# The odd layer's scans and the way to their projection: tiles placed by lifetime, squares and roots moved into waits, heads released one by one

## The reference

```python
amat = eye(L) + dec_strict * (k @ k.T) * b            # unit lower triangular
u0 = solve(amat, v); w = solve(amat, exp(g) * k)
pmat = dec_incl * (q @ k.T) * b
u = u0 - w @ S                                        # S: the state carried into the chunk
o = exp(g) * (q @ S) + pmat @ u
S = exp(g_last) * S + (exp(g_last - g) * b * k).T @ u
```

## Time and profile before

| | us |
|---|---|
| median of 3 runs | 1511.68 |
| lowest and highest | 1505.21, 1513.31 |
| profiled execution | 1506.36 |
| its span in the trace | 1504.2 |
| TensorE, VectorE, ScalarE, GpSimd busy | 1316.4, 527.8, 339.2, 112.3 |

### The profile page before, as it was taken

The page is one execution under the profiler, slowest core; times in us unless marked ns, Lnnn a source line. Parts: engine busy times, 40 slices in busy tenths (PEclk is TensorE's granted clock), DMA queues, the critical chain, the costliest instruction groups (busy, mean ns, idle before and its releaser), DMA issues.

```text
span 1504.2 us, 17094 instructions
## 1 busy us (share of the span) xinstructions
PE 1316.4 (88%) x6506; PEld 815.0 (54%) x6506; DVE 527.8 (35%) x1090; ACT 339.2 (23%) x724; POOL 112.3 (7%) x136
## 2 busy tenths in 40 slices
PE   6999788999998997888999997978877989987883
PEld 3554675466884333333565557878776843333332
DVE  3010473332234111011557817677662341101014
ACT  2100314333231111111336213221223311111111
POOL 2400010000001111110000000000000011111100
PEclk9999897999999999999999999999797999999997
DMA  9951666166537999997342200100007379999971
GB/s 362 332 180 58 223 152 246 68 238 240 222 139 296 390 415 418 418 417 311 122 152 72 85 0 1 29 1 1 1 18 287 137 294 411 413 418 418 417 287 63
DMA packets 80726, 329.12 MB, mean 219 GB/s; under 512 B 18383, under 2 KB 19577, under 8 KB 55936
## 3 DMA queue, kind: packets, MB, share of 16 engines
q1 hardware_dynamic: 66224, 300.54, 51.3%
q0 software_dynamic: 14416, 27.41, 5.7%
HBM read 320.04 MB, written 29.53 MB: 232 GB/s over the span
## 4 chain that ended last, share of the span: by engine, by line
PE 63%; DMA 15%; DVE 13%; issue 6%; ACT 2%; SPq 0%; POOL 0%; DVEq 0%; ACTq 0%; POOLq 0%
PE psum L921 20%; PE psum L1266 12%; PE psum L1015 9%; DMA arena<-in_moe_w_up 6%; PE psum L1292 5%; PE psum L947 3%; DMA wide<-in_moe_w_up 3%; DMA ring<-in_moe_w_up 3%; PE psum L1010 2%; DMA ring<-in_ada_w 2%; DVE arena L2381 2%; DVE wide L2341 1%; PE psum L890 1%; DMA arena<-h_rows,slot_token 1%; PE psum L954 1%
## 5 line engine op out<-in xcount | busy, mean ns | idle before, releaser
L921 PE MATMUL psum<-wide,ring 128*128 128x384 f32 x704 | 240.6, 502 | 3.8 <-ACT wide L1580 1.9
L921 PEld LDWEIGHTS psum<-wide,ring 128*128 128x128 f32 x704 | 165.6, 239 | 70.9 <-issue 9.5
L1266 PE MATMUL psum<-arena 128*64 128x512 f32 x480 | 151.6, 624 | 19.0 <-DMA ring<-in_moe_w_up 11.7
L1266 PE MATMUL psum<-ring,arena 128*64 128x512 f32 x384 | 134.4, 624 | 8.9 <-DMA wide<-in_moe_w_up 4.7
L1015 PE MATMUL psum<-ring 128*128 128x128 f32 x872 | 114.6, 290 | 18.0 <-issue 8.7
L1015 PEld LDWEIGHTS psum<-ring 128*128 128x128 f32 x872 | 108.9, 203 | 23.2 <-issue 13.4
L921 PE MATMUL psum<-ring,wide 128*128 128x512 f32 (+2 forms) x336 | 116.1, 507 | 0.0
L2252 DVE TENSOR_TENSOR arena<-arena,psum 128x256 f32<-128x256 f32 x34 | 14.3, 421 | 286.7 <-ACT arena L1728 286.7
L1266 PEld LDWEIGHTS psum<-arena 128*64 128x64 f32 x480 | 47.0, 144 | 96.6 <-issue 96.4
L1266 PE MATMUL psum<-wide,arena 128*64 128x512 f32 x224 | 88.1, 610 | 7.5 <-DMA arena<-in_moe_w_up 7.5
L921 PEld LDWEIGHTS psum<-ring,wide 128*128 128x128 f32 x336 | 58.3, 190 | 57.2 <-issue 56.4
(11 more groups left out here) (505 smaller groups left out, 1717.5 us busy)
## 6 DMA issues: line engine op xcount, KB each, us to landing
ring<-in_ada_w SPq DMA_DIRECT2D x23, 2048.0 KB, 13.0
arena<-in_moe_w_gate SPq DMA_DIRECT2D x28, 1024.0 KB, 14.0
arena<-in_moe_w_up SPq DMA_DIRECT2D x28, 1024.0 KB, 20.4
arena<-in_moe_w_down SPq DMA_DIRECT2D x28, 1024.0 KB, 20.8
ring<-in_moe_w_gate SPq DMA_DIRECT2D x24, 1024.0 KB, 13.7
ring<-in_moe_w_up SPq DMA_DIRECT2D x24, 1024.0 KB, 18.8
ring<-in_moe_w_down SPq DMA_DIRECT2D x24, 1024.0 KB, 20.9
ring<-in_w_in_odd SPq DMA_DIRECT2D x7, 2048.0 KB, 8.5
```

The source lines that it names most:

```text
L921: ins = mm(out, lhs(k), rhs(k), start=(k == 0), stop=(k == n - 1))
L1266: ins = mm(psum[half, 2 + s, :].rearrange("p (w f) -> p w f", w=2), hg[s][:, k, half], buffers[UNITS[q][h] % BUFFERS][0][:, :, k, :], star ...
```

## The change

- The tiles are dealt anew. `passing` is ring slots 1 and 2, `lasting` the arena part and ring slot 0. G, E1, xdt, xw, EB and (all in slots 1 and 2) Uw and AT are passing; XT, X, LT, TT, Rg, U, y2 and PT are lasting. The first half of the output weights (slot 1) waits for both Y1 of the third pair to be read, the second (slot 2) for the 36th LT, the last.
- KS and O2 of the third pair move from step 6 to step 5; in both pairs the two KS come before the two O2. VectorE's part for O2 (`carried_out`) comes after the subtraction of step 6 in the second pair, and in step 6 ahead of it in the third.
- VectorE gates ysum ahead of O1's additions. ScalarE squares the first token tile's heads in step 3 of the third pair and takes their root in step 4; it squares ysum after the U copies, and the heads of tiles 2 and 1 each after its O1 addition.
- VectorE scales the first tile's heads before the second root; the other eight go head by head, and each head of both tiles releases one group of transposes.

```diff
@@ plan_jobs, the odd layer's pairs
-            elif n == 6 and c:
-                jobs += [(name, u) for u in two for name in ("KS", "O2")]
+            elif n == (6 if pair < 2 else 5) and c:
+                jobs += [(name, u) for name in ("KS", "O2") for u in two]
@@ build, tiles of the scans
-        parts = (carve(4096), ring[:, 0, :], ring[:, 1, :], ring[:, 2, :])
-        G = [parts[2 * w][:, 0:1024] for w in range(2)]
-        E1, xdt, xw, y2, EB, PT = ([parts[2 * w][:, 512 * n:512 * n + 512] for w in range(2)] for n in range(2, 8))
-        AT, XT, X, LT, TT, Rg, U, Uw = ([parts[2 * w + 1][:, 512 * n:512 * n + 512] for w in range(2)] for n in range(8))
+        passing, lasting = (ring[:, 1, :], ring[:, 2, :]), (carve(4096), ring[:, 0, :])
+        G = [passing[w][:, 0:1024] for w in range(2)]
+        E1, xdt, xw, EB = ([passing[w][:, 512 * n:512 * n + 512] for w in range(2)] for n in range(2, 6))
+        Uw, AT = ([passing[n][:, 512 * w:512 * w + 512] for w in range(6, 8)] for n in range(2))
+        XT, X, LT, TT, Rg, U, y2, PT = ([lasting[w][:, 512 * n:512 * n + 512] for w in range(2)] for n in range(8))
@@ SyncE, load(n)
                 if (kind, what) == ("out", (1, 0)):
-                    sp.wait_ge(S("odd_sums"), 1)
+                    for u in (4, 5):
+                        sp.wait_ge(*taken("Y1", u))
+                if (kind, what) == ("out", (1, 1)):
+                    sp.wait_ge(S("lt"), 36)
@@ TensorE, pairs
-                        elif n == 6 and sequence:
+                        elif n == (6 if moves_on else 5) and sequence:
...
                             four(b, lambda h: conv[:, 12 + h, cols(c)], lambda h: Sg[:, 1, d, tok(h)])
+                    if n == (6 if moves_on else 5) and sequence:
+                        for u, d, c in two:
                             four(issue("O2", u), lambda h: conv[:, 8 + h, cols(c)], lambda h: Sg[:, 1, d, tok(h)])
@@ TensorE, mT
-                pe.wait_ge(S("odd_rows"), 1 if f < 4 else 2)
+                pe.wait_ge(S("odd_rows"), 1 if f < 4 else f - 2)
@@ ScalarE
+            scratch = skip[:, 0, :]
+            def gdn_squares(c):
+                for h in range(4):
+                    done(fn(scratch[:, 0:P], ogsum[:, c, h * P:(h + 1) * P], ACT.Square,
+                            accum_out=ms12[:, 4 * c + h:4 * c + h + 1]), "act_own")
...
+                    if pair == 2 and n == 3:
+                        gdn_squares(0)
+                    if pair == 2 and n == 4:
+                        fn(ms12[:, 0:4], ms12[:, 0:4], ACT.Sqrt, scale=1.0 / DK, bias=eps[:, 0:1])
                 for u, d, c in two:
                     act.wait_ge(*computed("U", u))
                     take(fn(U[d], bank("U", u), ACT.Copy), "U", u)
+                if pair == 2:
+                    for c in range(TILES):
+                        act.wait_ge(S("odd_sums"), c + 1)
+                        done(fn(scratch, ysum[:, c, :], ACT.Square, accum_out=ms3[:, c:c + 1]), "act_own")
...
-            scratch = G[0][:, 0:512]
-            for c in range(TILES):
-                act.wait_ge(S("odd_sums"), c + 1)
-                done(fn(scratch, ysum[:, c, :], ACT.Square, accum_out=ms3[:, c:c + 1]), "act_own")
             done(fn(ms3, ms3, ACT.Sqrt, scale=1.0 / 512, bias=eps[:, 0:1]), "roots")
-            for c in range(TILES):
-                for h in range(4):
...
-            done(fn(ms12, ms12, ACT.Sqrt, scale=1.0 / DK, bias=eps[:, 0:1]), "roots")
+            for u in (4, 5):
+                act.wait_ge(*taken("O1", u))
+                gdn_squares(units[u][1])
+            done(fn(ms12[:, 4:12], ms12[:, 4:12], ACT.Sqrt, scale=1.0 / DK, bias=eps[:, 0:1]), "roots")
@@ VectorE, pairs
+                def carried_out(u, d, c):
+                    og = ogsum[:, c, :]
+                    dve.wait_ge(*computed("O2", u))
+                    dst = og if first(d, c) else y2[d]
+                    take(tt(heads(dst, 4), heads(bank("O2", u), 4), b4(ecb[:, d, c, 8:12]), ALU.mult), "O2", u)
+                    if not first(d, c):
+                        o_(tt(og, og, y2[d], ALU.add))
...
-                        elif n == 6 and sequence:
+                        elif n == (6 if moves_on else 5) and sequence:
                             dve.wait_ge(*computed("KS", u))
...
-                            dve.wait_ge(*computed("O2", u))
...
+                        elif n == 6 and sequence:
+                            carried_out(u, d, c)
...
+                if sequence and moves_on:
+                    for u, d, c in two:
+                        carried_out(u, d, c)
+                if not moves_on:
+                    for c in range(TILES):
+                        done(tt(ysum[:, c, :], ysum[:, c, :], zs[:, c, :], ALU.mult), "odd_sums")
@@ VectorE, after the pairs
-            for c in range(TILES):
-                done(tt(ysum[:, c, :], ysum[:, c, :], zs[:, c, :], ALU.mult), "odd_sums")
             shift_products(1)
-            dve.wait_ge(S("gate_gain"), 1)
             dve.wait_ge(S("odd_in"), 64)
             dve.wait_ge(S("roots"), 3)
             o_(v.reciprocal(ms3, ms3))
+            o_(v.reciprocal(ms12[:, 0:4], ms12[:, 0:4]))
...
             done(ins, "odd_rows")
+            dve.wait_ge(S("gate_gain"), 1)
...
+            for h in range(4):
+                gated(0, h)
             dve.wait_ge(S("roots"), 4)
-            o_(v.reciprocal(ms12, ms12))
...
+            o_(v.reciprocal(ms12[:, 4:12], ms12[:, 4:12]))
+            for h in range(4):
+                gated(1, h)
+                done(gated(2, h), "odd_rows")
```

More of the change, by code:

```diff
@@ L2456, in _ @@
                             done(tt(Rg[d], gv[:, c, :], Rg[d], ALU.subtract), "rhs")
-                            dve.wait_ge(*computed("O2", u))
-                            dst = og if first(d, c) else y2[d]
-                            take(tt(heads(dst, 4), heads(bank("O2", u), 4), b4(ecb[:, d, c, 8:12]), ALU.mult), "O2", u)
-                            if not first(d, c):
-                                o_(tt(og, og, y2[d], ALU.add))
+                        elif n == 6 and sequence:
+                            carried_out(u, d, c)
                     for u, d, c in two:
@@ L2516, in _, with gated @@
             done(ins, "odd_rows")
-            dve.wait_ge(S("roots"), 4)
-            o_(v.reciprocal(ms12, ms12))
-            for c in range(TILES):
-                for h in range(4):
-                    at_ = slice(h * P, (h + 1) * P)
-                    ins = stt(ogsum[:, c, at_], ogsum[:, c, at_], ms12[:, 4 * c + h:4 * c + h + 1], zg[:, c, at_],
-                              ALU.mult, ALU.mult)
-            done(ins, "odd_rows")
+            dve.wait_ge(S("gate_gain"), 1)
+            def gated(c, h):
+                at_ = slice(h * P, (h + 1) * P)
+                return stt(ogsum[:, c, at_], ogsum[:, c, at_], ms12[:, 4 * c + h:4 * c + h + 1], zg[:, c, at_],
+                           ALU.mult, ALU.mult)
+            for h in range(4):
+                gated(0, h)
+            dve.wait_ge(S("roots"), 4)
+            o_(v.reciprocal(ms12[:, 4:12], ms12[:, 4:12]))
+            for h in range(4):
+                gated(1, h)
+                done(gated(2, h), "odd_rows")
             before_experts(1)
```

2 lines of the change are left out of this document (removed).

## The result

The changed kernel takes 1497.4 us (median of 7 runs, 1493.14 to 1500.43), the kernel before 1511.16 in its 7 runs. The ratio is 0.9909, with an interval of 0.9888 to 0.9931: 13.8 us faster, where the sum had 13.4. The profiled execution took 1497.4, its span is 1495.2.

A forecast was written before the change was run, and what follows sets the result against it. The prediction took the chain from the odd layer's scans to its output projection, ahead of the weight-bound expert stage, as what counts; 0.8 + 10.6 + 2.0 = 13.4 us, naming 1497 us, range 1488 to 1507.

The forecast's parts named there:

- second pair's hole: Second pair, step 6: VectorE subtracts before multiplying O2, so TensorE's hole of 0.78 goes; 0.8 us, bounds 0 and 0.8.
- step 5 to U, third pair: Third pair: KS and O2 products in step 5, VectorE's work under TensorE's, U starts earlier; gain 1.35 us.
- U to the projection: First U product to first projection product: faster clock over U and O1, shorter ScalarE and VectorE chain; gain 9.25 us.
- first projection block: First projection block: clock back up when the projection starts; gain 2.0 us, bounds 0 and 2.0.
- ScalarE's chain: First tile's squares, table load and root, 3.3 us, hidden in steps 3 and 4; ysum's root done by 1121.7.
- Heads one by one: Before the projection: eight heads released one at a time, so the second four transposes follow the first at once.
- The clock: U and O1 take 3.8 us instead of 5.45 after a shorter hole; clock back at the projection, gain 2.0.
- Weights: Output weight loads ahead of the projection: asked for late they would still land by 1128 to 1129.5; priced at 0.
- Rival 2: Weights a hidden bound, early arrival gives later work room: 14.8 with full-clock transposes, time 1496; counted in the forecast's range.
- Rival 1: Steps 3 to 6: step 6 doesn't shrink and squares delay a copy; gain 6.7, time 1504; 0.19 with rival 4.
- Rival 3: Eight projection blocks at 1.2 GHz: net loss 30.6 with all eight, time 1541; chance 0.05.
- Rival 4: Something between projection and expert stream keeps its own time; gain halved, 1504; chance 0.19 together with rival 1.

The follow-up runs named there:

- e3: Kernel after with KS and O2 back in step 6, their VectorE work ahead of the subtraction, both pairs: ratio 0.9918, U to projection 15.6 us.
- e10: Kernel before with the change to KS and O2 alone: ratio 0.9946, U to projection 22.6 us, first block 5.52.
- e5: Kernel after with the first tile's head squares and root back behind ysum's root, one reciprocal for twelve heads: ratio 0.9909, U to projection 18.7 us.
- e6: Kernel after, but the second four transposes wait for the last head: ratio 0.9927, U to projection 15.5 us, first block 7.52.
- e7: Kernel after with VectorE's three gatings of ysum behind O1's additions: ratio 0.9923, U to projection 17.1 us.
- e12: Kernel after profiled once more, unaltered: ratio 0.9890, U to projection 14.3 us, first block 5.53.
- e8: Kernel after with three dummy products ahead of the transposes: ratio 0.9882, U to projection 13.9 us, first block 7.22.
- e1: Kernel after with the output weights asked for at the old place, after the first gating of ysum: ratio 0.9918, U to projection 16.7 us.
- e2: Kernel before with only the tiles dealt anew and the weights asked for early: ratio 0.9996, U to projection 24.2 us.
- e9: Kernel after with three dummy products, and the first projection block waiting for each transposed group by itself: ratio 0.9873, first block 5.45 us.
- e4: Kernel before with six dummy products ahead of the first transposes and three ahead of the fifth: ratio 0.9974, first block 5.52 us.

## Why the prediction was right

Taken between fixed points of the two traces, each term of the sum has its measurement:

| term | forecast | measured in after | where |
|---|---|---|---|
| second pair's hole | 0.8 | 0.78 | shown by e3, e10 |
| step 5 to U, third pair | 1.35 | 1.52 (15.07 to 13.55) | shown by e3, e10 |
| U to the projection | 9.25 | 8.8 (24.0 to 15.2) | parts by e3, e5, e6, e7; 9.7 in e12 |
| first projection block | 2.0 | 2.06 | same in e12, but by the clock's odds |
| sum | 13.4 | 13.2 | ratio: 13.8 |

That the sum meets the ratio so closely is in part luck: with e12 for after it would be 14.1, the block's 2.0 came whole where about 1 was to be expected (below), and the ratio's interval alone is 10.4 to 16.9.

**The reading of the stage** held: what starts the projection sooner starts everything behind it sooner. From the end of the first block to the end of the trace it is 354.8 us in before, 352.5 in after and 356.0 in e12, and between 351.0 and 356.0 in all fourteen.

**KS and O2.** Right in mechanism, that TensorE's work only changes step and VectorE's goes under it. The bank wait, put at 0.1 and hidden, is there (0.30 in the weight load, 0.1 between products) and hidden behind VectorE's O2 work.

**ScalarE's chain.** Root at 1121.7 on the forecast's scale, where U stood at 1116.4: 5.3 after U; measured 5.32 (1122.00 to 1127.32). The load's 1.28 was hidden in step 4, with 4.25 to spare. The transposes began 8.1 after U in e12, as forecast, and 8.55 in the first trace. The 0.46 between them lie on VectorE: the router's copy (line 2332), which waits for TensorE's sixteen small products behind O1, ended 0.5 after the root there and held the reciprocals. I hadn't counted that wait; it is there in one execution and not in the other. The low bound of my sum was too mild in one place: with U and O1 at the low clock ScalarE starts on ysum's rows 1.6 later (4.38 after U in e3, 2.76 in after) and not 1.05. The Trainium skill (ScalarE: Activation LUTs, what ACT_TABLE_LOAD costs) splits the 2.7 us that the prediction quotes into about 1.28 for the load and about 1.38 for a drain. The traces agree on the load, 1.28 in each; a drain doesn't show in before, where the load starts 0.02 after the last square is read and the root 0.01 after the load.

**Heads one by one.** The second four transposes followed the first without a hole, as forecast, and e6 prices the edit at 1.2.

**The clock.** The measured times are what I took (3.99 for U and O1, 5.53 for the block), but they are of two kinds. Over U and O1 the low clock came with the hole of 2.23 in each of four traces and with 0.34 in none of ten. It didn't fall in that hole, though, as the prediction reads it: in before the granted clock is 1.00 from 1115.5 to 1117.75 and is lost about 1.1 us into the U products. The block's 2.0 I had treated as following from the work ahead of it, and its low clock in before as the result of two short bursts in 18 us; e10 and e8 show that it doesn't follow surely. By the counts above (five of seven against one of seven slow, at 1.3 to 2.1 each) it is worth about 1 on average (an estimate from these counts), and it came out whole. Besides, the clock over Y1 and the products behind it differs between executions of one program. Between the traces of before and after it makes 4.1 us (43.98 from step 1 to step 5 against 39.86), which isn't counted for either kernel. The Trainium skill (TensorE: Matmul & The Clock Gate, the part on what is happening) has activity lift the clock, and the traces agree as far as the odds go.

**Weights.** This is the step that failed, though it cost the sum nothing, since the kernel has the weights early. I put their part at 0 since, at the old place in the code, they would "be there by 1128 to 1129.5, just before 1131.2". e1 has them there 15.3 after they were asked for, not 10 to 12. The term is 0 in the kernel before (e2) and 1.5 of the 8.8 in the kernel after, up to 3.8 with the clock behind the hole. The 10.1 in rows 8 is a median of two loads that ran together, and I read it as the time of both: one landed after 7.8 and the other after 12.5, at 1137.7, 4 us ahead of the projection and not six. Rival 2 ("a hidden bound") was thus nearer to the truth than its text: hidden until the rest was faster, as I wrote at the end of the prediction's part on the weights. But where I saw room of 1.7 to 3.2 us, the weights come 2.4 too late in e1.

**The other rivals.** Rival 1 (cover too thin) falls with the 4.25 left ahead of the copy and the 1.52 gained ahead of U. Rival 3 (clock down through the projection): in all fourteen profiles the clock was up by the second block. Rival 4 (the gain lost behind the projection) falls with the ratio.

## What to carry to other kernels

Several short waits of different engines in a row are one chain: move what doesn't depend on the last result under the engine that is busy before it, and give the next engine each piece as it is done. A load that has room in the kernel before must be measured against the new time of its first use, with the landing of the last piece and not the median; its edit can be worth nothing alone and still be needed. For parts of a kernel that are below its spread between executions, fix two points in the trace and compare these lengths; a ratio of 0.3% precision can't see them.

## What the runs showed of the hardware

The granted clock differed between two profiles of the same program at the same place: Y1 of the last pair took 2 x 1.97 us in one and 6.55 in the other, the transposes 5.35 in one piece and 1.56 + 2.81. The 32 products of U and O1 took 5.4 to 5.6 us in each of four profiles with a hole of 2.23 ahead, and 3.99 in each of ten with 0.34. Dummy products ahead of the transposes didn't settle the clock behind them: in e8 the next block took 7.22, in e9 5.45.

One load of 2 MB alone landed 7.5 to 7.7 us after its issue in after. Two issued together landed after 7.8 to 8.2 and 12.5 to 13.0 (before, e4, e10), so that their median of 10.1 to 10.6 was the time of neither, and after 9.0 and 14.6 in e1, where a 512 KB load from another queue came in while they ran. Loads into the scan's tiles at a DMA share of 1.04 left the scan's steps as long as without (15.08 and 15.07 us).
